# Bias rows and page gate: a new order of the first steps in a hybrid decoder layer on one core

## The chip, the cores and the metric

The kernel runs on one core of one Trainium2 chip. The metric is the device time of one execution in microseconds. Several engines run their own instruction streams beside each other and meet at semaphores: TensorE (matmul), VectorE, ScalarE, GpSimd (POOL in the profile) and SyncE (SP), which here only issues DMAs. POOL and SP each feed a DMA queue of their own.

## What is computed

One inference step of one decoder layer, for a prompt of 512 tokens and 8 single sampled tokens, width 1024:

```python
def layer_forward(x, c, lw, rel_bias, past):
    sh1, sc1, gt1, sh2, sc2, gt2 = ada_mod(c, ada_w, ada_b)
    h = rmsnorm(x, norm1_g) * (1.0 + sc1) + sh1
    xr, yg, q, kv_c, kv_s, kv_w, gl = split_columns(h @ w_in)
    ...   # nsa_prompt / nsa_sample: three attention branches, with rel_bias added to all logits
    ...   # causal_conv, rg_lru, gelu(yg)
    mixed = jnp.concatenate([rmsnorm(o_lru, out_norm_lru), rmsnorm(o_att, out_norm_att)], axis=-1) @ w_out
    x = x + gt1 * mixed
    h2 = rmsnorm(x, norm2_g) * (1.0 + sc2) + sh2
    ff = peer_ffn(h2.reshape(B * T, D_MODEL), peer_wq, peer_bq, peer_subkeys, peer_u, peer_v)
    return x + gt2 * ff.reshape(B, T, D_MODEL), ...
```

The compressed attention branch of the sampled tokens reads 64 cache pages, found through a page table, and sends them through a small two-layer network. `rel_bias` is a table of 32 buckets by 8 heads; a distance picks the bucket.

## The kernel before

Everything is in float32, with the tokens (520) along the free dimension. Each engine has its own hand-written order of work.

**Head.** The modulation is computed from `ada_w` in steps. The first four, `ADA_HEAD`, take 2 MB blocks (`load_head`), the other 32 take 0.5 MB blocks (`load_tail`). A step is: TensorE multiplies (`ada_step`, L576, signals `ada_ready`), ScalarE copies out (`copy_m9`, L1107, `m9_ready`), TensorE turns the result (`turn_m9`, L586, `mt_ready`), VectorE adds the bias (`shift_m`, L1385, `mt_done`). Between the steps lies the first RMS norm: ScalarE squares x, TensorE sums (`strip_sums`, L556, `sum_ready`), VectorE inverts (`inverse_strips`), ScalarE takes the root (`rstd_ready`), TensorE spreads it (`spread_roots`, L563 and L564), VectorE multiplies x by it (L1394) and then scales and shifts (L1381, `h_ready`). In the kernel before, the sums come ahead of turning step 0 and doing step 1, the spreading ahead of turning step 1 and doing step 2.

**Projection.** For n = 0 to 17 TensorE computes z(n), a block of 128 columns of h @ w_in (L691, `z_ready`); `w_in` blocks come through two buffers, loaded by SP. Behind z(0) come `gate_strips` (L651) and `bias_rows` (L658 to L661), which multiplies `rel_bias` with the one-hot tables `ohd` and `oha` (33 partitions). ScalarE copies the bias rows to `rsb` and `tofs` and signals `act_init` 3; from there POOL stores them to the scratch tensors in DRAM (L474, L478, L481) and loads them back later for the attention. From n = 2 on, each z(n) is followed by two of the small modulation steps.

**Pages.** The 64 pages, 128 KB each, go to `xpool`. A page needs its number read from the table, so the issuing engine does `page_rows` (L281 and L282) one page at a time. SP issues pages 0 to 19: eight before n = 2 and four each at n = 2, 3 and 4. POOL issues pages 20 to 63, gated by `ada_ready` 3. Behind z(4) TensorE runs `hidden_pages` (L605), which waits for all 64 pages. SP's queue goes on with `w_in`, tails, the window keys `kwin` (2 MB, at n = 4), and from n = 7 on pages of the selection cache.

Behind that come the attention (to about 400 us) and the PEER part, the largest share of the span (L960 and L1064).

Of the kernel before, what the change touches and what calls it, by code (L numbers as in the profile page):

```python
# [20 lines left out]
P = 128  # L21
# [60 lines left out]
def build(nc, io):  # L82
    ctx = ExitStack()
    with ctx:
# [65 lines left out]
        def at(off, *shape):  # L150
# [101 lines left out]
            u_s pc_s u_tdone pc_t pc_tdone o_done u_p u_t u_pv mix_sq mix_ready proj_ready pe_step q_moved  # L252
            s_free s_ready tr_in tr_ready tr_done oh_ready ff_ready act_step root_in rstd_ready lru_prep
            exp_ready yg_ready pc_exp u_max u_exp u_rs hi_done rexp rexp_done dve_step hg_done gidx_ready
            roots_ready buckets_loaded hh_ready hl_ready ttr_done zg_gelu acc_step mul_done ah_done bank_free pages_k pages_s act_init pe_turned pe_init""".split()
        S = {n: sem(n) for n in names}
        ada_l = [sem(f"ada_loaded{i}") for i in range(2)]
        head_l = [sem(f"ada_head_loaded{i}") for i in range(3)]
# [27 lines left out]
        def _(sp):  # L286
            def load(dst, src, s):
                sp.dma_start(dst, src).then_inc(s, 16)

            def load_head(g, slot):  # L290
                load(ada_head[slot].rearrange("p (c k) i -> p c (k i)", k=KD),
                     io["ada_w"][4 * g:4 * g + 4].rearrange("c p k i -> p c (k i)"), head_l[slot])
# [5 lines left out]
            load(par[:, 80:128], io["adab"], S["tables_loaded"])  # L298
            load(rb[0:32], io["rel_bias"], S["tables_loaded"])
            load_head(1, 1)  # L300
            load_head(2, 2)
            sp.wait_ge(S["ada_ready"], 1)
            load_head(3, 0)
            load(wgate, io["w_gate"], S["wgate_loaded"])
            load(oha[0:33], io["oha"], S["buckets_loaded"])
            load(ohd[0:33], io["ohd"], S["buckets_loaded"])
            sp.wait_ge(S["ada_ready"], 3)
            for n in range(2):
                load(win_w[:, n * KD:(n + 1) * KD, :], io["w_in"][n], w_l[n])
# [10 lines left out]
            def load_pages(a, b):  # L320
                for n in range(a, b):
                    page_rows(sp, xpool[:, n, :], io["pool_c"], n, S["gather_k"])
            load_pages(0, 8)
            load(w1p, io["w1p"], S["w1k_loaded"])
            load(posp, io["posp"], S["pos_loaded"])

# [7 lines left out]
            for n in range(2, ZC):  # L334
                sp.wait_ge(S["z_ready"], n - 1)
                load(win_w[:, (n % 2) * KD:(n % 2 + 1) * KD, :], io["w_in"][n], w_l[n % 2])
                if 2 <= n <= 4:
                    load_pages(4 * n, 4 * n + 4)
                if n >= 7:
                    sp.wait_ge(S["hid_ready"], 2)  # L340
                    for m in range(3 * (n - 7), min(3 * (n - 6), 32)):
                        page_rows(sp, sel[:, m, :], io["pool_s"], m, S["gather_s"])
                load_tail(2 * n - 4)
                load_tail(2 * n - 3)
                if n == 5:
                    load(ohw[0:33], io["ohw"], S["ohw_loaded"])
                if n == 4:
                    sp.wait_ge(S["h_ready"], KD)
                    load(kwin, io["win_kT"], S["x_loaded"])
                if n == 5:  # L350
                    sp.wait_ge(S["prep_done"], 4)
                    for e in range(2):
                        load(wlru[e * HD:(e + 1) * HD, :, e * HD:(e + 1) * HD],
                             io["wlru"][e], S["lruw_loaded"])

            sp.wait_ge(S["ada_ready"], ADA_ALL)
            load_w1(sp, 0, S["w1k_loaded"])
# [100 lines left out]
        def _(pool):  # L458
            def load(dst, src, s):
# [5 lines left out]
            pool.affine_select(out=ident[:, :], in_=ident[:, :], compare_op=ALU.not_equal, fill=1.0,  # L465
                               base=0, pattern=[[-1, P]], channel_multiplier=1).then_inc(S["pool_done"], 1)

            pool.wait_ge(S["page_loaded"], 16)
            pool.wait_ge(S["ada_ready"], 3)
            for n in range(20, 64):  # L470
                page_rows(pool, xpool[:, n, :], io["pool_c"], n, S["pages_k"])
                if n == 44:
                    pool.wait_ge(S["act_init"], 3)
                    pool.dma_start(rscratch, rsb[0:NH]).then_inc(S["scratch_stored"], 16)  # L474
            pool.wait_ge(S["scratch_stored"], 16)
            ob = io["obias"]
            for a in range(8):
# [63 lines left out]
        def _(pe):  # L541
# [84 lines left out]
                last.then_inc(S["ck_ready"], 1)  # L626
            pe.wait_ge(S["prep_done"], 3)
            for g in range(ADA_HEAD):
                if g == 1:
                    pe.wait_ge(S["act_init"], 2)  # L630
                    for k in range(KD):
                        last = strip_sums(0, hT, k, KD)
                    last.then_inc(S["sum_ready"], 1)
                if g == 2:
                    pe.wait_ge(S["rstd_ready"], 1)
                    spread_roots(1, 0)
                if g >= 1:
                    turn_m9(g - 1)
                pe.wait_ge(head_l[g % 3], 16 * (g // 3 + 1))
                aw = ada_head[g % 3].rearrange("p (c k) i -> p c k i", k=KD)  # L640
                ada_step(g, lambda k: aw[:, :, k, :], 512)
            turn_m9(ADA_HEAD - 1)

            def gate_strips():
# [6 lines left out]
                            last = mm(ps[32 * j:32 * j + 32, 6 + h, 0:HALF], wgate[:, 2 * j + kk, :],  # L651
                                      hT[:, 2 * j + kk, h * HALF:(h + 1) * HALF], start=(kk == 0), stop=(kk == 1))
                last.then_inc(S["zg_ready"], 1)

            def bias_rows():

                pe.wait_ge(S["buckets_loaded"], 32)
                mm(ps[0:NH, 4, 0:512], rb[0:33], ohd[0:33, 513:1025], start=True, stop=True)  # L658
                mm(ps[0:NH, 5, 0:128], rb[0:33], ohd[0:33, 1025:1153], start=True, stop=True)
                for w in range(KD):  # L660
                    last = mm(ps[:, 5, P + w * NH:P + (w + 1) * NH], oha[0:33, w * P:(w + 1) * P], rb[0:33], start=True, stop=True)  # L661
                last.then_inc(S["pe_init"], 1)

            def gate_sums():

# [13 lines left out]
            for n in range(ZC):  # L679
                pe.wait_ge(w_l[n % 2], 16 * (n // 2 + 1))  # L680
                if n >= 2:
                    pe.wait_ge(S["z_moved"], n - 1)
                if n == 6:
                    pe.wait_ge(S["ck_moved"], 2)
                if 8 <= n <= 15:
                    pe.wait_ge(S["ri_ready"], n - 7)
                for k in range(KD):
                    if n == 0:
                        pe.wait_ge(S["h_ready"], k + 1)
                    for h in range(2):  # L690
                        last = mm(ps[:, 2 * (n % 2) + h, 0:HALF], win_w[:, (n % 2) * KD + k, :],  # L691
                                  hT[:, k, h * HALF:(h + 1) * HALF], start=(k == 0), stop=(k == KD - 1))
                last.then_inc(S["z_ready"], 1)
                if n == 0:
                    gate_strips()
                    bias_rows()
                if n == 1:
                    pe.wait_ge(S["act_init"], 3)
                    gate_sums()
                if 7 <= n <= 13 and n % 2:  # L700
                    lru_gate(n, 0)
                if n == 5:
                    pe.wait_ge(S["gelu_ready"], 2)
                if n >= 2:
                    for i in (2 * n - 4, 2 * n - 3):
                        pe.wait_ge(ada_l[i % 2], 16 * (i // 2 + 1))
                        ada_step(ADA_HEAD + i, lambda k: ada_tail[i % 2][:, k, :], P)
                if 7 <= n <= 13 and n % 2:
                    lru_gate(n, 1)
                if n == 5:  # L710
                    values_pages()
                if n == 2:
                    pe.wait_ge(S["gates_ready"], 2)
                if n >= 3:
                    for i in (2 * n - 6, 2 * n - 5):
                        turn_m9(ADA_HEAD + i)
                if n == 4:
                    hidden_pages(0)
                    hidden_pages(1)
                    keys_pages()  # L720
# [376 lines left out]
        def _(act):  # L1097
# [25 lines left out]
            fn(hT, xT[:, :, :], ACT.Square).then_inc(S["act_init"], 1)  # L1123
            copy_m9(1)
            root(1, roots)
            copy_m9(2)
            copy_m9(3)

# [12 lines left out]
                gelu_pages(1)  # L1141

            act.wait_ge(S["zg_ready"], 1)
            act.wait_ge(S["pe_init"], 1)
            fn(gT.rearrange("p (h t) -> p h t", h=2), ps[:, 6:8, 0:HALF], ACT.Copy).then_inc(S["gates_ready"], 1)
            link(fn(rsb[0:NH, 0:512], ps[0:NH, 4, 0:512], ACT.Copy), fn(tofs, ps[:, 5, P:P + KD * NH], ACT.Copy))
            fn(rsb[0:NH, 512:640], ps[0:NH, 5, 0:128], ACT.Copy).then_inc(S["act_init"], 1)

            act.wait_ge(S["scratch_stored"], 16)
            for n in range(1, ZC):  # L1150
# [180 lines left out]
        def _(dve):  # L1331
# [50 lines left out]
            def shift_m(i):  # L1382
# [1 line left out]
                c0, n = (4 * i, 4) if i < ADA_HEAD else (i + 3 * ADA_HEAD, 1)  # L1384
                tt(mT[:, c0:c0 + n, :], ps[:, 6 + i % 2, 0:9 * n].rearrange("p (q c) -> p q c", c=9),  # L1385
                   par[:, ADB + c0:ADB + c0 + n].to_broadcast([P, n, 9]), ADD).then_inc(S["mt_done"], 1)
            dve.wait_ge(S["tables_loaded"], 48)
            link(cp(rbx[0:33].rearrange("p (b h) -> p b h", h=NH),
                    rb[0:33].rearrange("p (o h) -> p o h", o=1).to_broadcast([33, P // NH, NH])))
            shift_m(0)  # L1390
            dve.wait_ge(S["sum_ready"], 1)
            inverse_strips(D, 0)
            dve.wait_ge(S["roots_ready"], 1)
            link(tt(hT[:, :, 0:SEQ], xT[:, :, 0:SEQ], ps[:, 1:2, 0:SEQ].to_broadcast([P, KD, SEQ]), MUL),  # L1394
                 tt(hT[:, :, SEQ:TOK], xT[:, :, SEQ:TOK], ps[:, 0:1, 256:256 + NB].to_broadcast([P, KD, NB]), MUL))
            for i in range(1, ADA_HEAD):
                shift_m(i)
            dve.wait_ge(S["mt_done"], ADA_HEAD)
            whole_scale(1, N1G)
            shifted(hT, 0)  # L1400
# [660 lines left out]
```

## Time and profile before

| | |
|---|---|
| median of 3 runs | 1851.92 us (1849.44 to 1853.21) |
| the profiled execution's own time | 1851.92 us |
| its span in the profile | 1850.1 us |
| TensorE busy | 1755.8 us (95%) |
| VectorE, ScalarE, GpSimd busy | 1317.2, 646.4, 350.5 us |
| moved by DMA | 467.88 MB, 253 GB/s in the mean |

Times in the trace count from the start of the span. A line such as L691 is a line of the kernel; where a helper issues the instruction, the line is that of the helper.

### The profile page before, as it was taken

How to read it: one execution, taken by the hardware profiler on the slowest of the kernel's cores; microseconds unless marked ns; L12 is line 12 of the kernel's file. 1: busy time of each engine (PE TensorE's matmuls, PEld its weight loads, DVE VectorE, ACT ScalarE, POOL GpSimd, SP SyncE). 2: the span in 40 equal slices, each digit the busy share in tenths (PEclk: the TensorE clock that was granted, in tenths of full speed). 3: DMA queues.
4: the chain of work that ended last, by engine and by line, in shares of the span. 5: the costliest groups of instructions: out<-in, count | busy, mean ns of one | idle time of the engine just before them, and what ended most of it. 6: DMA issues, size and time to landing. Idle time of an engine off the chain costs nothing.

```text
span 1850.1 us, 30371 instructions
## 1 busy us (share of the span) xinstructions
PE 1755.8 (95%) x11385; PEld 1633.9 (88%) x11385; DVE 1317.2 (71%) x2982; ACT 646.4 (35%) x1020; POOL 350.5 (19%) x390
## 2 busy tenths in 40 slices
PE   5999998789889999999999999999999999999997
PEld 3868876447789989999899999999999999999997
DVE  2102434663387789999899999994787777777776
ACT  2103422662132233334333343333333333333332
POOL 1512010000000001111233333332222222222220
PEclk8999996799899999999999999999999999999998
DMA  8948572500333226877799999999999999999992
GB/s 299 311 141 267 202 228 78 197 1 1 134 134 94 78 83 243 285 244 225 227 331 355 350 337 342 347 347 358 404 376 340 342 330 342 340 340 335 341 310 76
DMA packets 176606, 467.88 MB, mean 253 GB/s; under 512 B 20457, under 2 KB 90089, under 8 KB 174820
## 3 DMA queue, kind: packets, MB, share of 16 engines
q1 hardware_dynamic: 130532, 290.36, 45.3%
q0 software_dynamic: 45952, 175.97, 26.7%
q8 instruction: 68, 1.11, 0.2%
q14 instruction: 54, 0.44, 0.1%
HBM read 408.89 MB, written 64.17 MB: 256 GB/s over the span
## 4 chain that ended last, share of the span: by engine, by line
PE 83%; DVE 8%; DMA 3%; issue 2%; ACT 2%; POOLq 1%; POOL 0%; SPq 0%; DVEq 0%; ACTq 0%
PE ps L1064 29%; PE ps L960 25%; PE ps L691 5%; PE ps L1045 5%; PE ps L947 4%; PE ps L900 3%; PE ps L605 2%; ACT arena L1107 2%; PE ps L876 1%; PE ps L576 1%; DVE ul L1712 1%; PE ps L868 1%; DVE arena L1589 1%; DMA xT<-in_xT 1%; POOLq L281 1%
## 5 line engine op out<-in xcount | busy, mean ns | idle before, releaser
L1712 DVE TENSOR_TENSOR ul<-raw,uh 128x1024 fp32r<-128x1024 f32 x256 | 311.7, 1223 | 134.7 <-ACT uh L1107 118.2
L960 PE MATMUL ps<-hh,uh 128*128 128x392 f32 x1024 | 359.2, 351 | 5.3 <-DVE ul L1712 5.2
L960 PE MATMUL ps<-hl,uh 128*128 128x392 f32 x1024 | 350.5, 342 | 0.0
L960 PE MATMUL ps<-hh,ul 128*128 128x392 f32 x1024 | 349.5, 341 | 0.0
L1064 PE MATMUL ps<-ah,uh 128*128 128x392 f32 x1000 | 340.0, 340 | 3.0 <-DVE al L1921 3.0
L1064 PE MATMUL ps<-ah,ul 128*128 128x392 f32 x1000 | 342.1, 342 | 0.0
L1064 PE MATMUL ps<-al,uh 128*128 128x392 f32 x1000 | 341.4, 341 | 0.0
L1107 ACT ACTIVATE uh<-raw 128x1024 fp32r<-128x1024 f32 x256 | 270.2, 1055 | 123.8 <-PE ps L1064 103.6
L510 POOL DMA_INDIRECT xT<-in_u,gidx x128 | 147.5, 1152 | 584.8 <-DVE zg L1759 359.8
L510 POOL DMA_INDIRECT xT<-in_v,gidx x128 | 132.6, 1036 | 418.3 <-DVE vacc L1911 384.5
L1107 ACT ACTIVATE zbuf<-ps 128x392 f32<-128x392 f32 x128 | 63.7, 498 | 402.2 <-PE ps L960 355.5
L960 PEld LDWEIGHTS ps<-hh,uh 128*128 128x128 f32 x1024 | 193.9, 189 | 8.3 <-DVE ul L1712 6.6
L960 PEld LDWEIGHTS ps<-hl,uh 128*128 128x128 f32 x1024 | 193.9, 189 | 0.0
L960 PEld LDWEIGHTS ps<-hh,ul 128*128 128x128 f32 x1024 | 193.7, 189 | 0.0
L1064 PEld LDWEIGHTS ps<-ah,uh 128*128 128x128 f32 x1000 | 188.3, 188 | 3.3 <-issue 3.3
L1064 PEld LDWEIGHTS ps<-al,uh 128*128 128x128 f32 x1000 | 188.1, 188 | 0.0
L1064 PEld LDWEIGHTS ps<-ah,ul 128*128 128x128 f32 x1000 | 188.1, 188 | 0.0
L1911 DVE SCALAR_TENSOR_TENSOR vacc<-xT,ag,vacc 128x1024 f32<-128x1024 f32 x127 | 162.4, 1279 | 0.0
L1759 DVE CUSTOM_DVE_ANT_0 xT<-xT,hg 128x1024 f32<-128x1024 f32 x128 | 155.8, 1219 | 5.0 <-DMA xT<-in_u,gidx 5.0
L1107 ACT ACTIVATE ah<-zin 128x392 fp32r<-128x392 f32 x128 | 68.2, 533 | 227.6 <-DVE zin L1918 227.6
L691 PE MATMUL ps<-arena 128*128 128x260 f32 x576 | 135.2, 394 | 3.4 <-DVE arena L1381 2.0
L691 PEld LDWEIGHTS ps<-arena 128*128 128x128 f32 x576 | 111.3, 196 | 21.4 <-issue 4.2
(352 smaller groups left out, 2240.0 us busy)
## 6 DMA issues: line engine op xcount, KB each, us to landing
raw<-in_uT SPq DMA_DIRECT2D x128, 512.0 KB
raw<-in_v SPq DMA_DIRECT2D x128, 512.0 KB
zs<-zbuf SPq DMA_DIRECT2D x128, 196.0 KB
gw<-stage POOLq DMA_DIRECT2D x28, 896.0 KB
gr<-gw SPq DMA_DIRECT2D x32, 784.0 KB, 8.1
zin<-zs SPq DMA_DIRECT2D x128, 196.0 KB
arena<-in_ada_w SPq DMA_DIRECT2D x32, 512.0 KB, 4.6
arena<-in_w_in SPq DMA_DIRECT2D x18, 512.0 KB, 6.3
```

The lines of the kernel that those rows point to most:

```text
L510: pool.indirect_dma_start(out=gb[:, s, :], out_offset=None, in_=table, in_offset=bass.IndirectOffsetOnAxis(ap=gidx[:, n:n + 1], axis=0)).t ...
L605: mm(ps[g * HD:(g + 1) * HD, b + h, 1 - m:257 - m], w1p[:, c * 16 + m * 8 + j, :], xv[:, h, :, c, g, j, :], start=(m == 0 and j == 0), sto ...
L691: last = mm(ps[:, 2 * (n % 2) + h, 0:HALF], win_w[:, (n % 2) * KD + k, :], hT[:, k, h * HALF:(h + 1) * HALF], start=(k == 0), stop=(k == K ...
L900: last = mm(ps[:, 2 + 2 * (c % 3) + h, 0:HALF], wout[:, k, c * P:(c + 1) * P], zT[:, k, h * HALF:(h + 1) * HALF], start=(k == 0), stop=(k ...
L947: last = mm(ps[:, b + h, 0:HALF], weights[w](k), moving[m](k)[:, h * HALF:(h + 1) * HALF], start=(first and n == 0 and w == 0 and m == 0), ...
L960: last = mm(ps[:, bank, 0:DN], w[x][:, k * P:(k + 1) * P], m[:, k, G0:TOK], start=(k == 0 and x == 0 and m is hh), stop=(k == KD - 1 and x ...
L1045: last = mm(ps[:, 4 + n % 4, t * P:(t + 1) * P], oh[:, n % 6, t * P:(t + 1) * P], oh[:, n % 6, (4 + t) * P:(5 + t) * P], start=True, stop= ...
L1064: last = mm(ps[:, dc, 0:DN], w[:, q, cols], m[:, q, :], start=(first and w is uh and m is ah), stop=False)
L1107: return act.activation(out, in_, f, **kw)
L1712: tt(ul[:, i % 4, :], raw[:, i % 4, :], uh[:, i % 4, :].bitcast(F32), SUB).then_inc(S["lo_done"], 1)
L1759: dve.tensor_tensor_reduce(gb[:, n % 4, :], gb[:, n % 4, :], hg[:, :], 1.0, 0.0, MUL, ADD, zg[:, n:n + 1]).then_inc(S["ttr_done"], 1)
L1911: stt(vacc[:, :], gb[:, n % 4, :], ag[:, n:n + 1], vacc[:, :], MUL, ADD).then_inc(S["acc_step"], 1)
```

## The change

The bias rows, their tables and their store to scratch move from behind z(0) into the head; the head's order on TensorE changes; POOL's pages start behind another step; SP issues pages, tails and selection pages in another order.

```diff
@@ SP
             load_head(1, 1)
+            load(oha[0:33], io["oha"], S["tables_loaded"])
+            load(ohd[0:33], io["ohd"], S["tables_loaded"])
             load_head(2, 2)
             sp.wait_ge(S["ada_ready"], 1)
             load_head(3, 0)
             load(wgate, io["w_gate"], S["wgate_loaded"])
-            load(oha[0:33], io["oha"], S["buckets_loaded"])
-            load(ohd[0:33], io["ohd"], S["buckets_loaded"])
...
-            load_pages(0, 8)
+            load_pages(0, 12)
...
             for n in range(2, ZC):
                 sp.wait_ge(S["z_ready"], n - 1)
                 load(win_w[:, (n % 2) * KD:(n % 2 + 1) * KD, :], io["w_in"][n], w_l[n % 2])
-                if 2 <= n <= 4:
-                    load_pages(4 * n, 4 * n + 4)
-                if n >= 7:
-                    sp.wait_ge(S["hid_ready"], 2)
-                    for m in range(3 * (n - 7), min(3 * (n - 6), 32)):
-                        page_rows(sp, sel[:, m, :], io["pool_s"], m, S["gather_s"])
-                load_tail(2 * n - 4)
-                load_tail(2 * n - 3)
+                if n == 2:
+                    load_tail(0)
+                    load_tail(1)
+                    load_pages(12, 16)
+                if n == 3:
+                    load_pages(16, 20)
                 if n == 5:
                     load(ohw[0:33], io["ohw"], S["ohw_loaded"])
+                if n >= 3:
+                    load_tail(2 * n - 4)
+                    load_tail(2 * n - 3)
...
+                if n < 7:
+                    continue
+                sp.wait_ge(S["hid_ready"], 2)
+                for m in range(3 * (n - 7), min(3 * (n - 6), 32)):
+                    page_rows(sp, sel[:, m, :], io["pool_s"], m, S["gather_s"])
@@ POOL
+            pool.wait_ge(S["act_init"], 3)
+            pool.dma_start(rscratch, rsb[0:NH]).then_inc(S["scratch_stored"], 16)
             pool.wait_ge(S["page_loaded"], 16)
-            pool.wait_ge(S["ada_ready"], 3)
+            pool.wait_ge(S["ada_ready"], ADA_HEAD)
             for n in range(20, 64):
                 page_rows(pool, xpool[:, n, :], io["pool_c"], n, S["pages_k"])
-                if n == 44:
-                    pool.wait_ge(S["act_init"], 3)
-                    pool.dma_start(rscratch, rsb[0:NH]).then_inc(S["scratch_stored"], 16)
@@ TensorE
             for g in range(ADA_HEAD):
-                if g == 1:
+                if g >= 1:
+                    turn_m9(g - 1)
+                if g == 2:
                     pe.wait_ge(S["act_init"], 2)
                     for k in range(KD):
                         last = strip_sums(0, hT, k, KD)
                     last.then_inc(S["sum_ready"], 1)
-                if g == 2:
+
+                    pe.wait_ge(S["tables_loaded"], 80)
+                    mm(ps[0:NH, 2, 0:512], rb[0:33], ohd[0:33, 513:1025], start=True, stop=True)
+                    mm(ps[0:NH, 3, 0:128], rb[0:33], ohd[0:33, 1025:1153], start=True, stop=True)
+                    for w in range(KD):
+                        last = mm(ps[:, 3, P + w * NH:P + (w + 1) * NH], oha[0:33, w * P:(w + 1) * P], rb[0:33], start=True, stop=True)
+                    last.then_inc(S["pe_init"], 1)
+                if g == 3:
                     pe.wait_ge(S["rstd_ready"], 1)
                     spread_roots(1, 0)
-                if g >= 1:
-                    turn_m9(g - 1)
...
+                if n == 1:
+                    pe.wait_ge(S["act_init"], 3)
...
                 if n == 0:
                     gate_strips()
-                    bias_rows()
                 if n == 1:
-                    pe.wait_ge(S["act_init"], 3)
                     gate_sums()
@@ ScalarE
             copy_m9(1)
             root(1, roots)
+            act.wait_ge(S["pe_init"], 1)
+            link(fn(rsb[0:NH, 0:512], ps[0:NH, 2, 0:512], ACT.Copy), fn(tofs, ps[:, 3, P:P + KD * NH], ACT.Copy))
+            fn(rsb[0:NH, 512:640], ps[0:NH, 3, 0:128], ACT.Copy).then_inc(S["act_init"], 1)
             copy_m9(2)
             copy_m9(3)
...
             act.wait_ge(S["zg_ready"], 1)
-            act.wait_ge(S["pe_init"], 1)
             fn(gT.rearrange("p (h t) -> p h t", h=2), ps[:, 6:8, 0:HALF], ACT.Copy).then_inc(S["gates_ready"], 1)
-            link(fn(rsb[0:NH, 0:512], ps[0:NH, 4, 0:512], ACT.Copy), fn(tofs, ps[:, 5, P:P + KD * NH], ACT.Copy))
-            fn(rsb[0:NH, 512:640], ps[0:NH, 5, 0:128], ACT.Copy).then_inc(S["act_init"], 1)
@@ VectorE
-            dve.wait_ge(S["tables_loaded"], 48)
+            dve.wait_ge(S["tables_loaded"], 80)
...
             shift_m(0)
+            shift_m(1)
             dve.wait_ge(S["sum_ready"], 1)
             inverse_strips(D, 0)
             dve.wait_ge(S["roots_ready"], 1)
...
-            for i in range(1, ADA_HEAD):
-                shift_m(i)
+            shift_m(2)
+            shift_m(3)
```

The function `bias_rows` is gone; its matmuls stand in the loop over g, in banks 2 and 3 instead of 4 and 5.

## Rows read from the trace of the kernel before

**Rows 1.** Chain of waits, first 100 us: start, us, what.

```profile
34.70 0.50 POOLq L281
...
87.27 9.37 DMA arena<-in_pool_c
...
96.89 3.22 PE ps L605 x13
```

**Rows 2.** Timeline of TensorE ahead of L605: start, us, instructions.

```profile
91.94 0.59 PE L586 MATMUL ps<-arena 128*128 128x9 f32 x4
```

**Rows 3.** Waits of TensorE, 96 to 340 us: total, times, longest.

```profile
PE ps L853 <- DVEq L1643: 3.4, 1, 3.4
```

**Rows 4.** Timelines of TensorE, ScalarE, VectorE and POOL in the head.

```profile
19.65 3.85 PE L556 MATMUL ps<-arena,ones 128*32 128x136 f32 x64 [5.50 <-ACT arena L1107]
...
23.43 1.26 PE L586 MATMUL ps<-arena 128*128 128x9 f32 x8
...
26.62 0.60 ACT L1107 ACTIVATE arena<-ps 128x512 f32<-128x512 f32 x1 [7.02 <-PE ps L576]
...
28.90 1.16 PE L563 MATMUL ps<-arena,ident 128*128 128x128 f32 x8 [2.35 <-ACT arena L1107]
...
30.21 4.42 DVE L1394 TENSOR_TENSOR arena<-xT,ps 128x4096 f32<-128x4096 f32 x1 [3.96 <-PE ps L564]
...
31.21 3.35 PE L576 MATMUL ps<-arena 128*32 128x512 f32 x16
...
36.18 0.59 POOL L282 DMA_DIRECT2D arena<-in_pool_c  x1 [33.62 <-issue]
...
36.27 1.92 PE L576 MATMUL ps<-arena 128*32 128x512 f32 x16
...
40.01 0.20 DVE L1385 TENSOR_TENSOR mT<-ps,par 128x36 f32<-128x36 f32 x1 [3.44 <-PE ps L586]
...
41.95 0.77 PE L691 MATMUL ps<-arena 128*128 128x260 f32 x1 [1.98 <-DVE arena L1381]
```

**Rows 5.** Groups of POOL's instructions, 34 to 97 us.

```profile
L282 POOL DMA_DIRECT2D arena<-in_pool_c x44 | 24.1, 548 | 60.6 <-issue 60.6
```

**Rows 6.** DMA issues, 3 to 4.2 us: size, us to landing.

```profile
arena<-in_ada_w SPq DMA_DIRECT2D x1, 2048.0 KB, 17.3
```

**Rows 7.** Windows of TensorE: us, busy, granted clock, DMA share, GB/s.

```profile
20.00:21.00 1.00, 1.00 (x24) 0.50 1.07 430
...
60.00:61.00 1.00, 1.00 (x4) 0.50 1.08 383
```

**Rows 8.** Timeline of TensorE, 53 to 75 us.

```profile
53.91 1.02 PE L658 MATMUL ps<-arena,cst 33*8 33x512 f32 x2
...
56.96 8.97 PE L691 MATMUL ps<-arena 128*128 128x260 f32 x32
...
66.81 7.28 PE L691 MATMUL ps<-arena 128*128 128x260 f32 x32
```

**Rows 9.** DMA issues at 82.7, 83.9, 87.2 and 83.8 us: us to landing.

```profile
arena<-in_pool_c POOLq DMA_DIRECT2D x1, 128.0 KB, 3.9
...
arena<-in_pool_c POOLq DMA_DIRECT2D x1, 128.0 KB, 7.3
...
arena<-in_pool_c POOLq DMA_DIRECT2D x1, 128.0 KB, 9.4
...
xT<-in_win_kT SPq DMA_DIRECT2D x1, 2048.0 KB, 12.0
```

**Rows 10.** DMA queues (SP's q1, POOL's q0), 84 to 96 us: packets, MB, share.

```profile
q1 hardware_dynamic: 667, 3.84, 78.9%
...
q0 software_dynamic: 401, 0.78, 21.5%
```

**Rows 11.** SP's timeline, 34 to 50 us, and a DMA issue at 52 us.

```profile
41.16 8.16 SPq L282 DMA_DIRECT2D arena<-in_pool_c  x8
...
arena<-in_w_in SPq DMA_DIRECT2D x1, 512.0 KB, 8.3
```

More of the change, by code:

```diff
@@ L254, in build @@
             exp_ready yg_ready pc_exp u_max u_exp u_rs hi_done rexp rexp_done dve_step hg_done gidx_ready
-            roots_ready buckets_loaded hh_ready hl_ready ttr_done zg_gelu acc_step mul_done ah_done bank_free pages_k pages_s act_init pe_turned pe_init""".split()
+            roots_ready hh_ready hl_ready ttr_done zg_gelu acc_step mul_done ah_done bank_free pages_k pages_s act_init pe_turned pe_init""".split()
         S = {n: sem(n) for n in names}
@@ L653, in gate_strips @@
                 last.then_inc(S["zg_ready"], 1)
[L655 to L662, printed above, removed]
             def gate_sums():
```

## The prediction

> **What bounds the kernel now.** The page comes first: TensorE is busy for 95% of the span and carries 83% of the chain that ended last. Nearly all of that lies behind the part that changes, so the question is by how much the first 97 us move. The chain of waits for the first 100 us says what sets them [rows 1]: from 34.70 us on it is POOL's queue, which prepares one cache page after another, then the landing of the last page, 87.27 + 9.37 = 96.64 us, and at 96.89 us TensorE starts `hidden_pages` (L605). TensorE waited for it: its last work before ends at 91.94 + 0.59 = 92.53 us [rows 2], so it has 4.36 us of slack there. Work taken off TensorE before 92.5 us is worth nothing unless the last page lands sooner.
>
> After 96.9 us TensorE's own work sets the pace: up to 340 us its longest wait for others is 3.4 us, on VectorE [rows 3], and none but that for the pages is on a DMA. So a shift of the start of `hidden_pages` passes to the end in full, and I count nothing else behind it.
>
> **Part 1, POOL's gate.** Before, the 44 page issues begin after `ada_ready` 3, the end of the third modulation step: 31.21 + 3.35 = 34.56 us [rows 4]. The first issue starts at 36.18 us, the last at 87.27 us: 51.09 us for 44 intervals, since the store of `rscratch` (L474) takes one, so 1.16 us each [rows 1, 4, 5]. From gate to last issue that is 52.71 us. After, the gate is `ada_ready` 4, and the store goes out ahead of it, as long as `act_init` 3 comes about 1.2 us earlier than that step's end; one interval is saved: 52.71 - 1.16 = 51.55 us. (The store needs only the bias rows and ScalarE's copies, which end some 7 us ahead of the gate by the sum below.) Before, the fourth step ended at 36.27 + 1.92 = 38.19 us, so the gate alone costs at least 3.63 - 1.16 = 2.5 us if the head keeps its times.
>
> **Part 2, the head in its new order.** TensorE now turns step 0, does step 1, turns it, and only then sums the squares, multiplies the bias rows, does step 2, turns it, spreads the roots, does step 3. Walking it:
> - Step 1 needs the second weight block, issued at 3.85 us and landed 17.3 us later: 21.15 us [rows 6]. Such a step costs 1.92 us at the high clock and 3.35 us at the low one [rows 4]. The clock stood at 0.50 when TensorE had been idle before 19.65 us and resumed work [rows 7]. It idles before 21.15 us again, so I take the low one: 24.5 us.
> - ScalarE's copy 0.60 and its handover: 25.2 us. Turning, 1.26 us at most: 26.4 us [rows 4].
> - The strip sums took 3.85 us at the low clock [rows 4]; at the high one I estimate half, 1.93 us; I take 2.3 us: 28.7 us.
> - Bias rows: L658, L659 and L661 ran from 53.91 us to the start of z(1) at 56.96 us, 3.1 us [rows 8]: 31.8 us. The new 33-row tables, 0.28 MB behind block 1 at some 0.4 MB per us, are there by about 22 us.
> - Step 2: between 1.92 and 3.35 us. After the bias rows of before the clock went to 0.50 although TensorE never idled (60 to 61 us [rows 7]), and the same matmuls now precede step 2. I take 2.6 us: 34.4 us.
> - Copy 0.7, turn 1.15, spreading 1.3 us [rows 4]: 37.6 us. The fourth block is no limit: step 3 of before started at 36.27 us without a wait for it, and it is issued behind the same event, the end of step 0.
> - Step 3, 1.92 to 3.35 us, taken as 2.2: **39.8 us**.
>
> With every open term at its low end it is 38.1 us, with every one at its high end (sums 3.85, both later steps 3.35, turns 1.26, spreading 1.45) 43.6 us; a low clock over the bias rows too would add up to 3.1. The gate thus moves from 34.56 to 39.8 us, +5.2, and the last page issue to 39.8 + 51.55 = **91.35 us**, against 87.27.
>
> **Part 3, landing.** A page took 3.9 us to land when issued at 82.7 us, then 7.3, and 9.4 for the last [rows 9]. The change of regime falls together with the load of `kwin`, 2 MB, issued on SP at 83.8 us and landed 12.0 us later [rows 9]. From 84 to 96 us POOL's queue moved 0.78 MB, 2 us per page of 0.13 MB, while SP's moved 3.84 MB [rows 10]: pages come in faster than they leave. The page issued at 83.9 us landed at 91.2, the last at 96.64 us: three pages later, so 1.8 us apart, though issued 1.16 us apart. `kwin` waits only for old steps of TensorE, so it stays near 83.5 us, and in the new kernel some three more pages have yet to be issued behind it. If the backlog keeps growing at 1.8 us for a page, 6.4 pages after the one of 83.9 us land at 91.2 + 11.5 = 102.7 us; if the delay stays at 9.4 us, 91.35 + 9.4 = 100.8 us. SP's four pages of 78 to 81.7 us are gone from there (they go out with z(1) to z(2)), which relieves it. I take 101.0 us, and with 0.25 us of issue `hidden_pages` starts at 101.3 us instead of 96.89: **+4.4 us**.
> The Trainium skill ("DMA: Bandwidth & Descriptors", section on queues, rings and completion order) has each DMA engine go round the queues that hold work, a packet at a time. By the packets of that stretch [rows 10], 2 KB against 5.8 KB, equal turns would give POOL's queue a quarter of the 4.62 MB moved in those 12 us, 1.35 us per page, and by an estimate from that the last page would land at about 99.9 us, 1855.2 us in all. The trace shows fewer turns for POOL than equal ones, so the sum does not use it.
>
> **Part 4, what the rest is worth.** The bias rows leave the stretch behind z(0): 3.1 us of TensorE, and perhaps the 1.7 us by which z(1) (8.97 us) exceeded z(2) (7.28 us) [rows 8]. z(0) itself starts later: the roots are spread at 37.6, VectorE's product takes 4.42 + 0.21 us, two shifts and the first scaling another 2.2 (40.01 to 41.95 us with one shift [rows 4]), so z(0) starts at about 44.4 us instead of 41.95. TensorE reaches `hidden_pages` at 92.53 + 2.45 - 3.1 = 91.9 us, or 90.2 with the clock's part: 9 us ahead of the pages. So both the gain of 3.1 to 4.8 us and the loss of 2.45 us are hidden behind POOL; if that cover were gone they would count -0.65 to -2.35 us together. SP issues 12 pages at 1.02 us from about 41.2 us on instead of 8, then four small loads (2.2 us), so `w_in` for z(2) goes out at about 55.8 us; if it takes 8.3 us to land as before, it is there at 64.1 us, and z(2) wants it at 66.81 + 2.45 - 3.1 = 66.2 us, or 64.5 with the clock's part [rows 8, 11]. The tail blocks ahead of pages, and ScalarE's wait for `scratch_stored`, which falls away, touch work that TensorE did not wait for. Of the selection pages, now behind the tails, the same holds: no wait for them stands among TensorE's up to 340 us.
>
> **Sum.** The profiled execution took 1851.92 us, the median of the three runs, so it is the base: 1851.92 + 4.4 = **1856.3 us**. By my bounds for the likeliest case (landing at 99.5 to 103 us) it is 1854.8 to 1858.3.
>
> **Rivals.**
> 1. The backlog drains. With fewer SP pages ahead and `kwin` nearly in (95 us), the last page may land as fast as those before 83 us: 91.35 + 3.9 + 0.25 = 95.5 us, 1.4 us sooner than before: 1850.5 us. For it: 3.9 us held until 82.7 us. Against it: two tail blocks (1 MB) go out near 91 us on SP behind an unfinished `w_in`. It decides once the delay is below 5.3 us. Chance 0.17.
> 2. The low clock holds through the head: gate at 43.6 us, last issue at 95.15, landing 9.4, start 104.8 us: +7.9, 1859.8 us. For it, step 2 of before ran low although TensorE had worked since 28.90 us, and the clock was low behind the bias rows; against, step 3 ran high soon after. Chance 0.13.
> 3. The pages do not bind, the change does what its order suggests, and TensorE sets the end of this stretch: start at 91.9 us, 5.0 us sooner: 1846.9 us. It would need the last page landed by 91.7 us, though even at the earliest gate of 38.1 us its issue starts at 89.65. Chance 0.05.
> 4. SP becomes the bound: a `w_in` or tail block late for z(2). It must be 9 us late before it shows; a delay of 11 us would give 1858.3 us. Chance 0.05.
>
> **How the numbers follow.** The forecast case has 0.6. This kernel's measurement can tell about 0.2%, 3.7 us, from no change. Of the forecast case some 0.42 lies above +3.7 us and 0.18 below; rivals 2 and 4 end almost wholly above, rival 1 within, rival 3 below -3.7. So slower 0.57, the same 0.37, faster 0.06. The range reaches from the middle of rival 1, 1850.5 us, to just past rival 2, 1861 us.
>
> **What would show it.** In the new profile: the fourth step's end near 39.8 us and the first page issue 1.6 us behind it (right if 38 to 44 us); 44 issues 1.16 us apart, the last near 91.4 us; its landing 8 to 11 us later; TensorE idle for about 9 us ahead of L605 instead of 4.4; z(1) at 7.3 to 9 us. The prediction is wrong if the last page lands in about 4 us, if the gate opens before 38 us, or if a stretch behind 97 us changes its length, which I rule out only from the waits of before.

## The result: slower by 0.67%, nearly three times the forecast

| | median | runs | ratio to before, 95% interval |
|---|---|---|---|
| before | 1851.0 us | 9 | |
| changed | 1862.6 us | 9 | 1.0067 [1.0055, 1.0081] |

That is about +12.4 us by the ratio; forecast were +4.4 us, and the range ended at 1861 us. The profiled execution of the changed kernel took 1861.52 us with a span of 1858.6 us, against 1851.92 and 1850.1.

The first stretch went nearly as forecast. The chain of waits of the changed kernel, 80 to 110 us (start, duration, what), answers to [rows 1]:

```profile
92.00 8.60 DMA arena<-in_pool_c
100.61 0.25 issue
100.85 9.24 PE ps L610 x57
```

The timelines of TensorE and POOL in its head answer to [rows 4] (L581 is the step, L561 the sums, L643 the first bias matmul):

```profile
21.36 3.50 PE L581 MATMUL ps<-arena 128*32 128x512 f32 x16 [5.22 <-DMA arena<-in_ada_w]
...
26.58 2.06 PE L561 MATMUL ps<-arena,ones 128*32 128x136 f32 x64
28.57 1.02 PE L643 MATMUL ps<-arena,cst 33*8 33x512 f32 x2
...
31.75 3.43 PE L581 MATMUL ps<-arena 128*32 128x512 f32 x16
...
38.01 1.93 PE L581 MATMUL ps<-arena 128*32 128x512 f32 x16
```

```profile
41.56 0.58 POOL L282 DMA_DIRECT2D arena<-in_pool_c  x1 [7.83 <-issue]
```

Step 3 ends at 39.94 us, the first page issue follows 1.62 us later, the last starts at 92.00 us and lands 8.60 us later. `hidden_pages` starts at 100.85 instead of 96.89 us, +3.96.

Ahead of that point TensorE had more trouble than forecast (timeline, 48 to 150 us; answers to [rows 2, 8]):

```profile
55.57 7.28 PE L696 MATMUL ps<-arena 128*128 128x260 f32 x32
...
66.56 10.14 PE L696 MATMUL ps<-arena 128*128 128x260 f32 x32 [2.76 <-DMA arena<-in_w_in]
...
94.55 0.60 PE L591 MATMUL ps<-arena 128*128 128x9 f32 x4
```

z(1) takes the 7.28 us hoped for. It does so in all six profiles with the new head, and takes 8.81 to 8.97 us in all six with the old one, where the bias rows stand before it. z(2) (at 66.56 us) waits 2.76 us for its weights and runs 10.14 us, mostly at the low clock. TensorE is done at 95.15 us, later than the forecast's 90.2 to 91.9, and pages still come last, by 5.71 us instead of some 9. The wait for them has a price of its own: the first 128 matmuls of `hidden_pages` take 16.81 us behind it, about as in before,

```profile
96.89 16.73 PE L605 MATMUL ps<-arena 128*64 128x256 f32 x128 [4.36 <-DMA arena<-in_pool_c]
```

while the granted clock stands at 0.50 from its start to 104 us; the second 128 take 14.03 us, and so do the first ones in profiles where TensorE hardly waits (a_gate3, a_both, b_sel_last, b_gate2 and b_gate1 below).

The rest of the loss lies behind 97 us, where the forecast had none. TensorE's longest waits, 14 to 340 us (in total, times, longest), answer to [rows 3]:

```profile
PE ps L696 <- DMA arena<-in_w_in: 8.1, 3, 4.4
PE ps L610 <- DMA arena<-in_pool_c: 5.7, 1, 5.7
```

Three waits for `w_in` blocks, where before had none: 2.76 us at z(2), 4.45 at z(8), 0.90 at z(17). Here is z(8) on TensorE (0.51 us of turning in front of it, then the wait in brackets):

```profile
166.81 0.51 PE L591 MATMUL ps<-arena 128*128 128x9 f32 x4
171.77 8.76 PE L696 MATMUL ps<-arena 128*128 128x260 f32 x32 [4.45 <-DMA arena<-in_w_in]
```

And SP's timeline in front of it (L288 issues plain loads, L282 pages), changed kernel first, then the kernel before around its own z(8), which started at 163.13 us without a wait:

```profile
155.98 0.80 SPq L288 DMA_DIRECT2D arena<-in_ada_w  x2
157.74 2.56 SPq L282 DMA_DIRECT2D arena<-in_pool_s  x3
160.34 0.43 SPq L288 DMA_DIRECT2D arena<-in_w_in  x1
```

```profile
151.94 0.81 SPq L288 DMA_DIRECT2D arena<-in_ada_w  x2
152.80 0.43 SPq L288 DMA_DIRECT2D arena<-in_w_in  x1
154.00 3.10 SPq L282 DMA_DIRECT2D arena<-in_pool_s  x3
```

The tails are the two `in_ada_w` blocks. SP can issue each of them only when TensorE has done a small step. In before, `w_in` follows 0.86 us behind them and the selection pages come third. In the changed kernel the pages come second, and `w_in` goes out 4.36 us behind the start of the tails: the three page issues take 2.56 us, and 0.96 us pass ahead of the first. It also took longer to land (DMA issues, changed at 160.3 us, then before at 152.8 us):

```profile
arena<-in_w_in SPq DMA_DIRECT2D x1, 512.0 KB, 11.4
```

```profile
arena<-in_w_in SPq DMA_DIRECT2D x1, 512.0 KB, 7.6
```

160.34 + 11.4 = 171.7 us, while z(8) could have started at 167.3 us. In before it was 152.80 + 7.6 = 160.4 us, 2.7 us ahead of need. Measured from `hidden_pages`, whose start moved by about 4 us, the block goes out 3.6 us later and takes 3.8 us more; less the 2.7 us of slack that is the wait, to within 0.3 us. The longer landing goes together with POOL's queue (its timeline, changed, then before: the weights of the value network):

```profile
160.42 1.08 POOL L278 DMA_DIRECT2D arena<-in_cmp_w  x2
```

```profile
156.37 1.08 POOL L278 DMA_DIRECT2D arena<-in_cmp_w  x2
```

In before these two 512 KB loads start 3.6 us behind the `w_in` block; now they start beside it. The later issue alone would hardly have been enough: with a landing of 7.6 us the block would be there at 167.9 us, 0.6 us late. The other profiles fit: the block lands in 6.4 to 7.6 us where these loads start behind it, and in 9.4 to 11.4 us where they start with it or up to 1.7 us ahead. But the latter are exactly the kernels with the pages in second place, so what POOL's loads add by themselves is not shown. After the pause z(8) takes 8.76 instead of 7.26 us. Comparing starts in the two traces: +3.96 us at `hidden_pages`, +8.64 at z(8), +10.13 at z(9), +11.19 at the transposes behind z(17) (267.20 against 256.01 us). In these two executions 2.7 us then come back (the spans differ by 8.5 us). TensorE's granted clock was higher in one stretch of the changed one, for a reason that the traces don't show; windows of 25 us from the same point of the value network on (us, busy time of PE, PEld, DVE, ACT and POOL, granted clock, DMA share, GB/s), before and changed. At clock 0.50 TensorE got through 289 matmuls, at 0.62 through 371:

```profile
276.80:302.00 25.20, 25.18 (x289) 22.17 (x288) 4.12 (x10) 5.40 (x10) 0.00 (x0) 0.50 0.02 4
```

```profile
288.20:313.30 25.10, 25.08 (x371) 20.86 (x370) 8.30 (x16) 5.41 (x10) 0.00 (x0) 0.62 0.01 3
```

So the profile shows two losses: the gate, near 4 us, and SP's order, near 7 us.

### The profile page after: what moved, and what is told of

Same layout as the page of the kernel before. It is cut to its first block, busy times and chain, and to the rows that moved or that the text cites. A ratio compares the mean times of both kernels' runs of the same rounds, so it can differ in the third digit from the quotient of the medians.

```text
span 1858.6 us, 30370 instructions
## 1 busy us (share of the span) xinstructions
PE 1756.1 (94%) x11385; PEld 1632.7 (88%) x11385; DVE 1317.1 (71%) x2982; ACT 647.8 (35%) x1020; POOL 393.2 (21%) x390
## 4 chain that ended last, share of the span: by engine, by line
PE 82%; DVE 7%; DMA 4%; issue 2%; ACT 1%; POOLq 1%; SPq 1%; POOL 0%; DVEq 0%; ACTq 0%
PE ps L1067 29%; PE ps L963 25%; PE ps L1048 5%; PE ps L950 4%; PE ps L696 4%; PE ps L903 3%; PE ps L610 2%; ACT arena L1110 1%; PE ps L879 1%; PE ps L581 1%; DMA arena<-in_w_in 1%; DMA arena<-in_ada_w 1%; PE ps L871 1%; DVE ul L1716 1%; PE ps L810 1%
## 5 line engine op out<-in xcount | busy, mean ns | idle before, releaser
L1716 DVE TENSOR_TENSOR ul<-raw,uh 128x1024 fp32r<-128x1024 f32 x256 | 316.5, 1242 | 130.0 <-ACT uh L1110 112.2
L515 POOL DMA_INDIRECT xT<-in_u,gidx x128 | 189.3, 1479 | 548.4 <-DVE zg L1763 320.6
L1763 DVE CUSTOM_DVE_ANT_0 xT<-xT,hg 128x1024 f32<-128x1024 f32 x128 | 162.9, 1274 | 11.3 <-DMA xT<-in_u,gidx 11.3
```

Of the source, the lines that this page charges most:

```text
L515: pool.indirect_dma_start(out=gb[:, s, :], out_offset=None, in_=table, in_offset=bass.IndirectOffsetOnAxis(ap=gidx[:, n:n + 1], axis=0)).t ...
L1716: tt(ul[:, i % 4, :], raw[:, i % 4, :], uh[:, i % 4, :].bitcast(F32), SUB).then_inc(S["lo_done"], 1)
L1763: dve.tensor_tensor_reduce(gb[:, n % 4, :], gb[:, n % 4, :], hg[:, :], 1.0, 0.0, MUL, ADD, zg[:, n:n + 1]).then_inc(S["ttr_done"], 1)
```

## The experiments

Medians are over 8 to 12 executions of each kernel, ratios against 19 to 35 executions of the kernel before on the same chip.

| kernel | median | ratio to before, 95% interval |
|---|---|---|
| a_sel_first | 1855.71 us | 1.0032 [1.0016, 1.0048] |
| a_gate3 | 1857.79 us | 1.0047 [1.0027, 1.0066] |
| a_both | 1848.41 us | 0.9995 [0.9979, 1.0011] |
| b_sel_last | 1858.64 us | 1.0047 [1.0030, 1.0064] |
| b_gate4 | 1855.76 us | 1.0032 [1.0018, 1.0046] |
| b_both | 1863.09 us | 1.0057 [1.0037, 1.0077] |
| c_gate3 | 1852.13 us | 1.0007 [0.9994, 1.0020] |
| c_gate2 | 1847.52 us | 0.9987 [0.9966, 1.0007] |
| b_gate2 | 1844.36 us | 0.9980 [0.9966, 0.9995] |
| b_gate1 | 1847.06 us | 0.9975 [0.9960, 0.9990] |

**a_sel_first: the changed kernel, selection pages ahead of the tails again.**

```diff
+                if n >= 7:
+                    sp.wait_ge(S["hid_ready"], 2)
+                    ...   # three selection pages
                 if n >= 3:
                     load_tail(2 * n - 4)
                     load_tail(2 * n - 3)
...
-                if n < 7:
-                    continue
-                sp.wait_ge(S["hid_ready"], 2)
-                ...
```

> The changed kernel with one edit undone: from n = 7 on, SP issues the three selection pages ahead of the two tail blocks again, so that they stand before the wait for a modulation step and not between it and the next w_in block. Theory A (SP's order): the w_in block for z(8) goes out about 1 us behind the tails instead of 4.4 us, TensorE's wait of 4.45 us at z(8), its low clock there (8.76 instead of 7.26 us) and the 0.90 us at z(17) go away, so 5 to 7 us less than the changed kernel: 1855 to 1858 us. Theory B (only the page gate matters, and the wait at z(8) is DMA crowding by pages and weights of the value network that any order would meet): no change against the changed kernel, 1862 us, and the wait at z(8) stays.

1.0032 instead of 1.0067: about 6.5 us of the 12.4 are gone, in the medians (the profiled execution, 1860.45 us, is one of its slowest: its head ran at the low clock, and pages came late). SP's timeline has its old order back,

```profile
159.16 0.81 SPq L288 DMA_DIRECT2D arena<-in_ada_w  x2
160.02 0.43 SPq L288 DMA_DIRECT2D arena<-in_w_in  x1
161.22 2.92 SPq L282 DMA_DIRECT2D arena<-in_pool_s  x3
```

and z(8) follows at once (170.36 us, 7.26 us long). The same DMAs move the same bytes; only their order differs. Theory B falls.

In the names below, gate n is `ada_ready` n, the end of step n - 1.

**a_gate3: the changed kernel, page gate at step 2 again.**

```diff
-            pool.wait_ge(S["ada_ready"], ADA_HEAD)
+            pool.wait_ge(S["ada_ready"], 3)
```

> The changed kernel with POOL's page gate back at the third modulation step (ada_ready 3). The gate opens 4.8 us earlier (35.2 instead of 39.9 us), the last page issue falls at about 87.2 us and lands 9 us later at 96. Theory A (POOL's queue sets the first stretch): hidden_pages starts near 96.5 instead of 100.85 us and 3.5 to 4.5 us of the whole are gone, about 1858.5 us; the wait at z(8) stays. Rival (TensorE, late by w_in for z(2), sets it): TensorE arrives at 95.2 us, so no more than 5 us could be won; if its arrival or the landing moves with the earlier pages, less than 1 us is won.

1.0047: 3.7 us gone by the medians of the ratios, though this interval and that of the changed kernel overlap. The profile is clearer. Chain of waits, and the wait at z(8), which stays:

```profile
87.69 8.27 DMA arena<-in_pool_c
...
96.20 6.88 PE ps L610 x61
```

```profile
164.08 8.97 PE L696 MATMUL ps<-arena 128*128 128x260 f32 x32 [2.50 <-DMA arena<-in_w_in]
```

`hidden_pages` starts at 96.20 us, 4.65 us sooner than in the changed kernel. TensorE was done at 95.57 us, so it had nearly become the bound, and the first 128 matmuls of `hidden_pages` take 14.03 instead of 16.81 us. At z(6) 1.7 us are lost again (8.94 instead of 7.25 us, at the low clock).

**a_both: both edits.**

> The changed kernel with both edits: page gate at ada_ready 3, selection pages ahead of the tails. If the two causes add and are all there is, this stands within 2 us of the kernel before (ratio 0.999 to 1.001), with bias rows in the head. If a third cause is left, it stays 3 us or more slower than before.

0.9995: the whole loss is gone, with the new head, the bias rows in it and SP's new order of compressed pages still in place. A third cause of 3 us is ruled out by the interval (-3.9 to +2.0 us). This is so in the medians; the profiled execution gets there another way than before did. Its head ran low, z(2) waited 3.73 us for `w_in` and took 9.71 us, and TensorE came to `hidden_pages` at 101.20 us, behind the last page; without a wait for pages its first part took 14.03 us. The two edits are worth 13.3 us together, 10.2 us as the sum of the single ones; the intervals are too wide to call that an interaction.

**b_sel_last: the kernel before, selection pages behind the tails.**

> The kernel before with one edit of the change alone: the selection pages of n >= 7 are issued behind the tails and what follows them. Theory A: a wait for w_in appears at z(8) (about 4 us, with some 1.5 us of low clock behind it) and the whole grows by 5 to 7 us. Theory B: under 1 us, since TensorE never waited for these loads before.

1.0047, +8.7 us with an interval of 5.6 to 11.8, so rather more than expected. The wait appears in a kernel that never had it (L691 is z(8)):

```profile
165.00 8.97 PE L691 MATMUL ps<-arena 128*128 128x260 f32 x32 [3.32 <-DMA arena<-in_w_in]
```

3.32 us of wait and 1.71 us of low clock here, and 0.69 us at z(17), 5.7 us in all. The remaining 3 us of the median are within its interval; no trace accounts for them.

**b_gate4: the kernel before, page gate at step 3.**

```diff
-            pool.wait_ge(S["ada_ready"], 3)
+            pool.wait_ge(S["ada_ready"], 4)
```

> The kernel before with POOL's page gate moved from ada_ready 3 to ada_ready 4 and nothing else. Forecast's theory (each microsecond of the gate arrives at the end): the gate moves by 3.6 us, the last issue with it, the landing stays 8.5 to 9.5 us, so +3 to +4 us, ratio 1.0016 to 1.002. Rival (later pages land faster, since the window keys have drained): under +1 us.

1.0032, +5.9 us with an interval of 3.3 to 8.5. The profile has its last issue 3.87 us later and +3.28 us at `hidden_pages`; the landing takes 8.79 us, though the window keys went out at 84.07 us as in before and three more pages were issued behind them:

```profile
91.14 8.79 DMA arena<-in_pool_c
100.17 11.99 PE ps L605 x81
```

**b_both: both edits on the kernel before.**

> The kernel before with two edits of the change: gate at ada_ready 4 and selection pages behind the tails; head, bias rows and SP's compressed pages as before. Theory (these two edits are the whole loss, the new head is worth about nothing): ratio 1.006 to 1.009, as the changed kernel (1.0067). Rival (the losses overlap, or the head carries a loss of its own): under 1.005.

1.0057, with an interval that holds the changed kernel's 1.0067. The median falls just short of the 1.006 expected. Its profile has both waits, 6.63 us for the pages and 4.54 us for `w_in` at z(8), which then takes 10.10 us. Two edits out of the change reproduce its loss within what can be told.

**c_gate3: the new head alone.** This is the changed kernel with gate, store of the bias rows and SP's loop as before.

> The changed kernel's head alone (new order on TensorE, bias rows and their tables in it), with everything else as before: gate at ada_ready 3, the store of the bias rows inside POOL's pages, SP's pages, tails and selection pages in the old order. Forecast's part 4: gain and loss of the head are hidden behind POOL, so within 1 us of before plus the 0.6 us by which the third step ends later. Rival: the longer chain on TensorE ahead of the gate meets a low clock and moves the gate by 2 to 5 us in a good part of the executions, so +2 us or more in the median.

1.0007, no difference that can be told: the interval is -1.1 to +3.7 us. It agrees with Part 4's statement that the head's gains and losses are hidden, but it is too wide to show it, or to exclude the rival's 2 us. The rival's mechanism is real; in this profile, the second slowest of twelve (1856.9 us), three of the four steps (L583) take 3.64 us, wholly at the low clock (the first is not among these rows):

```profile
21.81 3.64 PE L583 MATMUL ps<-arena 128*32 128x512 f32 x16 [4.82 <-DMA arena<-in_ada_w]
...
37.49 3.64 PE L583 MATMUL ps<-arena 128*32 128x512 f32 x16
...
45.79 2.42 PE L583 MATMUL ps<-arena 128*32 128x512 f32 x16
```

Here the gate, step 2's end, is at 41.13 us, 6.6 us later than in before, and `hidden_pages` starts at 103.03 us.

**b_gate2 and b_gate1: the kernel before, page gate at step 1 or step 0.**

> The kernel before with the page gate at ada_ready 2, about 8 us earlier. If POOL's queue bounds the first 97 us, the pages land before TensorE arrives at 92.5 us and the 4.4 us of waiting go: -3 to -5 us, ratio 0.9973 to 0.9984. Rival: the pages now compete with the third and fourth weight block (the gate was a guard for them), the head ends 2 to 4 us later and nothing is won.

> The kernel before with the page gate at ada_ready 1. Theory: TensorE already binds this stretch with the gate at ada_ready 2, so the earlier gate wins nothing more, and pages issued from 16 us on crowd the second and third weight block; ratio 0.998 to 1.000, not better than with ada_ready 2 (0.998). Rival: POOL still binds in part of the executions, then 0.996 to 0.9975.

0.9980 and 0.9975: both beat the kernel before, and the changed one by 0.9%. Between themselves they can't be told apart, and their traces say why. The store of the bias rows stands inside POOL's pages (behind the page n = 44) and waits for `act_init` 3. With the gate at step 1 POOL stands there for 5.54 us,

```profile
61.63 0.56 POOL L474 DMA_DIRECT2D rscratch<-arena  x1 [5.54 <-ACT arena L1107]
```

and with the gate at step 0 for 17.62 us: the first page goes out at 16.46 instead of 27.41 us, the last at 85.08 instead of 84.11. So in the old kernel an earlier gate buys nothing beyond that store. With the bias rows in the head that stop is gone: c_gate2 issues its last page at 78.46 us.

In the profile of b_gate2 no wait for pages is left; z(4), its small step and its turns run straight into L605 (chain of waits):

```profile
86.60 7.11 PE ps L691 x32
93.72 1.01 PE ps L576 x32
94.73 0.54 PE ps L586 x4
95.27 13.96 PE ps L605 x128
```

That execution had three of its four steps at 3.64 us, the low clock, and still started `hidden_pages` 1.6 us before the kernel before. Another 2.7 us come from its first part, 14.0 us here against 16.73. So of the 4.4 us gained by z(8), which starts at 158.75 instead of 163.13 us, more than half is clock and not an earlier start. With the gate at step 0 the pages do crowd the fourth weight block: step 3 waits for it.

```profile
39.63 3.64 PE L576 MATMUL ps<-arena 128*32 128x512 f32 x16 [1.79 <-DMA arena<-in_ada_w]
```

**c_gate2: the new head with the gate at step 1.**

> The same with the gate at ada_ready 2. Pages land before TensorE arrives, which makes the head's gain visible: TensorE arrives at 90 to 92 us where the clock is kind, so -5 to -6.5 us against before, 0.5 to 2 us better than the kernel before with the same gate. Rival: the pages crowd out the third weight block and the low clock takes the rest: no better than before with that gate.

0.9987, its interval holds 1 and also that of b_gate2: a gain of 0.5 to 2 us over that kernel is neither shown nor excluded. What differs is the spread: 1840.4 to 1859.0 us over twelve executions, against 1841.2 to 1847.4 over ten of b_gate2. The profiled one is the slowest of the twelve. The rival's reason is not what it shows, since the third weight block is not waited for; it has a wait for tail blocks:

```profile
87.37 1.06 PE ps L583 x32
...
88.44 13.67 DMA arena<-in_ada_w
```

From 85 to 95 us POOL's queue moved 2.61 MB and SP's, which carries these blocks, 0.66 MB. With its pages done early, POOL had issued its next load, 2.5 MB of `rrows`, at 83.14 us, ahead of the tails; in b_gate2 that load goes out at 88.79 us and SP's queue moves 3.36 MB in the same stretch. Whether this makes the slow executions I did not find out; one trace can't say.

## Why the prediction was wrong

**What held.** The gate: 39.8 us forecast, 39.94 in the profile. That it is so close is in part luck, as the six profiles with this head show (below). The walk through the head: sums 2.3 us (measured 2.06), bias rows 3.1 (3.2), step 2 taken as 2.6 between bounds of 1.92 and 3.35 (3.43), step 3 as 2.2 (1.93). Last issue 91.35 (92.00). Landing taken as 9.65 us (8.60): the delay did not grow with the backlog. One premise was off here, since `kwin` went out at 86.40 us and not near 83.5, so that fewer pages stood behind it; in b_gate4, where it kept its place, the delay did not grow either. The last page landed at 100.6 us, forecast were 101.0. By the Trainium skill ("DMA: Bandwidth & Descriptors", queues, rings and completion order) equal turns for both queues gave an estimate of 99.9 us; the measured time lies between the two and tells neither apart. In all +4.4 us forecast, +3.96 in the profile, and the direction was right. b_gate4 and a_gate3 show that moving this gate moves the end: by 5.9 and 3.7 us in the medians.

**The step that failed** is the term that the sum put at nothing, all that lies behind `hidden_pages` ("I count nothing else behind it"), and its reason in part 4: "Of the selection pages, now behind the tails, the same holds: no wait for them stands among TensorE's up to 340 us." I asked who waits for the moved loads. Nobody does. I did not ask what is now queued behind them: SP works in order, the tails in front hold it until TensorE's small step is done, and the next `w_in` block, which in before went out in the next microsecond, now stands behind the page issues, 3.5 us with the pause ahead of them. That no wait for `w_in` stood in the trace of before was no proof of slack. The block of z(8) was issued at 152.80 us, landed 7.6 us later and was wanted at 163.13: 2.7 us of slack, readable in the trace of before, against 3.5 us put in front of it, and loads of POOL's that it now went out beside. a_sel_first takes 6.5 us out of the changed kernel, b_sel_last puts 8.7 us into the kernel before; the profile's account of the changed kernel gives 4.45 + 1.50 us at z(8) and about 1.1 us at z(17). Rival 4 had the right kind of cause (a `w_in` block late on SP) but only for z(2), where the wait for pages covered it.

**In z(2) itself** the forecast was also off: `w_in` went out at 57.61 us, not 55.8, because the 12 pages took 13.19 us to issue, not 12.2, and started later. It landed 8.9 us later, and TensorE stood for 2.76 us. With eight pages there, in c_gate3, z(2) does not wait. In the changed kernel nothing came of it, since the pages for `hidden_pages` were later still; with the gate earlier it starts to count (a_gate3, a_both).

**Rival 2, the low clock in the head,** is no either-or. It differs between executions: step 3 of the new head ended at 39.94, 40.37, 43.01, 45.57, 48.21 and 48.55 us in the profiles of the changed kernel, a_gate3, a_sel_first, a_both, c_gate3 and c_gate2, three of them past the 43.6 us of the forecast's high end. That high end was too low: a step wholly at the low clock takes 3.64 us, not 3.35, and in these three the first bias matmuls ran low too (1.87 instead of 1.02 us), which it left out. In the old head it ended at 38.19 us in before, 38.38 in b_gate4, 40.92 in b_gate2, 41.00 in b_sel_last and 41.55 in b_both. A gate behind a longer chain of TensorE work takes more of this into the median. That may be why the gate costs more in the medians than the 4 us of one profile. It was not measured separately.

## What to carry to other kernels

When a load is moved on a queue that works in order, list what comes after its new place up to the next wait, and compare each item's issue, landing and due time; the absence of a wait in the old trace says only that the slack was not negative. A gate at the head of a serial chain of issues (44 pages at 1.16 us) is worth its full delay until the chain stops being the bound, so look first for the earliest point at which it may open, and then for what stops the chain further on: here that one line gave 0.2 to 0.25%, the store of the bias rows capped it, and moving 3 us of matmul gave nothing that could be told. Loads that TensorE needs soon go ahead of loads that fill idle time, even if the latter cost only a microsecond each to issue.

## What the hardware showed beyond expectation

A pause ahead of a block has a second price, as the block after it runs partly at the low clock. Eight pauses of 1.41 to 4.54 us for `w_in` were followed by blocks of 8.76 to 10.14 us instead of 7.3, 1.5 to 2.9 us more, and the length of the pause doesn't order them (2.76 us: 10.14, 4.45 us: 8.76). One of 1.85 us, at z(17) in b_both, and those of up to 0.9 us cost nothing more. The waits for pages, 4.4 to 7.4 us, cost another 2.2 to 3.0 us in `hidden_pages`. So a wait that is taken away can give back more than its own length. The bias matmuls, 33 rows deep, were followed by a step at the low clock (3.43 us) in the changed kernel's profile without any idle time between them, as z(1) was in before. That they are the reason is not shown for the step: in the old head step 2 follows no bias rows, though an idle time of 2.35 us shortly before, and takes 3.35 to 3.64 us as well.

The granted clock of the head can't always be taken from the record. In the profile of a_both the windows read 1.00 where the step's 16 matmuls took 3.64 us, the time of the low level (windows: us, busy, clock, DMA share, GB/s; then timeline):

```profile
21.00:25.00 4.00, 3.35 (x16) 1.00 1.00 341
...
37.00:41.00 4.00, 3.81 (x18) 1.00 0.03 5
```

```profile
21.65 3.64 PE L580 MATMUL ps<-arena 128*32 128x512 f32 x16 [4.77 <-DMA arena<-in_ada_w]
...
37.34 3.48 PE L580 MATMUL ps<-arena 128*32 128x512 f32 x16
```

There the duration of a known instruction is the better witness.
